# A ten-stage transformer block on one core: the first adaLN sums taken by TensorE, constants loaded later, zeroing products removed

## The chip, the cores and the metric

The kernel runs on one core of a Trainium2 chip. The metric is device time in microseconds (us) of one execution. All operands are fp32 in HBM.

## The reference, cut to what matters

Ten layers follow each other on a 256 x 1024 activation: FFN, Mamba-2, FFN, FFN, MoBA attention, FFN, stick-breaking attention, convolutional FFN, sparse (DSA) attention, convolutional FFN. Each is preceded by a modulated RMSNorm whose shift, scale and gate are a product of one vector with a large matrix:

```python
c_act = jax.nn.silu(c)                       # one vector of 1024
m = c_act @ w + b                            # w is 1024 x 3072, one per stage
shift, scale, gate = jnp.split(m, 3, axis=-1)
h = rmsnorm(x, g) * (1.0 + scale[:, None, :]) + shift[:, None, :]
x = x + 0.5 * gate * ((jax.nn.silu(h @ w_gate) * (h @ w_up)) @ w_down)
```

Every weight product is made at nearly fp32 accuracy: weights and activations are split into a high and a low part (fp32r), and three products hi*hi, hi*lo, lo*hi are summed.

## The kernel before, in words

**Layout.** x lies transposed in SBUF (`x`, 128 x 8 x 256). Weights come as 277 blocks of 1 MB (`raw0` to `raw5`, six buffers). For each block ScalarE writes `w_hi` (L421), VectorE writes `w_lo = raw - w_hi` (L817), two blocks ahead of TensorE (`AHEAD`), and TensorE makes 48 products (L1371 to L1373). A FFN takes gate block, up block, down block in turn (eleven of each); gate and up go to PSUM banks 4 and 5, the down products of the whole stage are summed in banks 0 to 3 (`acc(m)`, two to a bank).

**Start of a stage.** `norm(st)` on ScalarE squares x (L437), TensorE sums the squares with a matrix of ones (L1431, bank 6), ScalarE makes `rstd` (L425, L427), VectorE writes `work` (L908), ScalarE `h_hi` (L449), VectorE `h_lo` (L913). The first product of a stage runs as these land (L1384, L1386, then L1391). Between, TensorE zeroes banks 0 to 3 with four bf16 products of zeros (L1446, 128x512 each), so that all down products can accumulate. After the first gate product there is a small fp32 product into bank 6 that nobody reads (L1468).

**The modulation.** VectorE sums c times the 1024 rows of w in chunks of 128 rows (`macc`), for stages 1 to 9 in the background of FFN stages (L845, L848), then transposes (L828), reduces (L831) and TensorE folds (L1423). For stage 0 it is done at the start, before any weight product: eight chunks of 1 MB into `first_mod` (L345; the first four at once, each later one when the buffer is free), eight sums on VectorE (L1340, L1343), two transposes, two reductions, one small product, four additions (L875). The gate part of stage 0 comes later: four 0.5 MB pieces on ScalarE's queue (L411), summed in `first_gate` (L857 to L867).

**Queues.** All large loads are on SyncE's queue, in the order in which they are written: eight mods chunks with x (1 MB) before the last, `con` (all constants, 974 KB), six `raw` blocks, four mods chunks of the next stage, and then one `raw` per block freed. ScalarE's queue carries `par` (all parameters, 1189 KB) first, and later the gate pieces.

```python
            for n in range(KT):
                if n >= 4:
                    eng.wait_ge(sems["mo"], n - 3)
                eng.dma_start(first_mod[n % 4], mods[n][:, 0:2048]).then_inc(s_mo[n % 4], 16)
                if n == KT - 2:
                    eng.dma_start(x[:, :, :], xin).then_inc(s_in, 16)
            eng.dma_start(con[:, :], consts).then_inc(s_con, 16)
```

Of the kernel before, what the change touches and what calls it, by code (L numbers as in the profile page):

```python
# [71 lines left out]
PARAMS, NPARAM = offsets(PARAM_COLS)  # L72
CONSTS, NCONST = offsets(CONST_COLS)
# [49 lines left out]
class Plan:  # L123
# [20 lines left out]
    def steps(self, st, kind):  # L144
        g = GROUPS[kind]
        out = {"fold": 4, "mods": 1, "modv": 1, "pair": 3, "xup": 8, "sq": 8, "ss": 1, "ln": 1, "rstd": 1,
               "t": 8, "hhi": 8, "hlo": 8, "zero": 1, "ahi": 0, "alo": 0}
# [60 lines left out]
def build(nc, weights, mods, params, consts, xin, out, stages=None):  # L208
# [3 lines left out]
    with ExitStack() as ctx:  # L212
# [36 lines left out]
        turned_first = [modws[:, 3072:4608], modws[:, 4608:6144]]  # L249
# [9 lines left out]
        sems = {n: sem(n) for n in list(plan.total) + ["blk", "whi", "wlo", "macc", "const", "cact", "xst", "mo", "go", "gmods"]}  # L259
# [4 lines left out]
        s_in, s_par, s_con, s_out, s_rel, s_bias = (sem(n) for n in ("in", "par", "con", "out", "relst", "bias"))  # L264
# [19 lines left out]
        zero_b = conb[:, 3 * P:4 * P]  # L284
# [55 lines left out]
        def _(eng):  # L340
            k = Steps(eng, plan, sems)
            for n in range(KT):
                if n >= 4:
                    eng.wait_ge(sems["mo"], n - 3)
                eng.dma_start(first_mod[n % 4], mods[n][:, 0:2048]).then_inc(s_mo[n % 4], 16)  # L345
                if n == KT - 2:
                    eng.dma_start(x[:, :, :], xin).then_inc(s_in, 16)
            eng.dma_start(con[:, :], consts).then_inc(s_con, 16)

            def load(g):  # L350

                if g < plan.nblk:
                    if g >= NRAW:
                        eng.wait_ge(sems["wlo"], g - NRAW + 1)
                    eng.dma_start(raw[g % NRAW][:, :], weights[g]).then_inc(s_raw[g % NRAW], 16)

            def load_mod(q):

                if q < 16 * (NST - 1):
                    if q < 4:  # L360
                        eng.wait_ge(sems["fold"], 4)
# [5 lines left out]
            for g in range(NRAW):  # L367
                load(g)
            for q in range(4):
# [16 lines left out]
        def _(eng):  # L386
            k = Steps(eng, plan, sems)
            eng.dma_start(par[:, :], params).then_inc(s_par, 16)
            eng.wait_ge(s_par, 16)
            k.inc("cact", eng.activation(cact[:, :], par_("c"), ACT.Silu))  # L390

            def start():

                eng.wait_ge(s_con, 16)
                eng.activation(ident_b, con_("ident"), ACT.Copy)
# [5 lines left out]
                for b in range(-AHEAD, 0):  # L401
                    split(0, b=b)
                gate_weights(0)
# [25 lines left out]
            def norm(st):  # L429
# [10 lines left out]
                if st == 0:  # L440
                    start()
# [5 lines left out]
                for m in range(KT):  # L447
                    k.wait("t", st, b=m)
                    k.inc("hhi", eng.activation(h_hi[:, m, :], work3[:, m, :], ACT.Identity,  # L449
                                                bias=modv[:, st, m:m + 1]))  # L450

            def ffn(st):
# [23 lines left out]
                for n in range(1, NFB):  # L476
# [3 lines left out]
                    if st == 0 and n == GATE_AT:  # L480
                        gate_weights(1)
# [316 lines left out]
        def _(eng):  # L798
# [4 lines left out]
            eng.memset(zero_b, 0.0)  # L803

            def more_constants():
                eng.wait_ge(s_con, 16)
                eng.tensor_scalar(below_b, con_("tri"), 1.0, -NEG, ALU.subtract, ALU.mult).then_inc(sems["xst"], 1)
                eng.wait_ge(sems["const"], 1)
                eng.tensor_tensor(ws_lo[:, :], par_("wsmall"), ws_hi[:, :], ALU.subtract).then_inc(sems["xst"], 1)
# [9 lines left out]

            def fold(j, n):  # L820

                if n == 0:
                    eng.wait_ge(sems["macc"] if j else sems["mo"], 16 * j or KT)
                half, w = n % 2, 1536 if j else 1024
                flat = (turned if j else turned_first)[half][:, 0:w]
# [8 lines left out]
            def gather(st, n, step):  # L834
# [5 lines left out]
                for q in mod_parts(st, n, step):  # L840
                    m, c = macc[:, 1536 * (q % 2):1536 * (q % 2 + 1)], cact[:, KT + q // 2:KT + q // 2 + 1]
                    eng.wait_ge(s_modw[q % 4], 16 * (q // 4) + 16)
                    if q % 16 < 2:
                        k.wait("fold", q // 16, b=q % 2)
# [34 lines left out]
            def modulation(st):  # L879
# [3 lines left out]
                ins = tiles(st, 0, 24 if st else 16, 0)  # L883
                ins.then_inc(sems["xst"], 1)
                eng.wait_ge(sems["xst"], 2 + 2 * st + 1)
# [3 lines left out]
                eng.wait_ge(sems["xst"], 2 + 2 * st + 2)  # L889
# [64 lines left out]
            def ffn(st):  # L954
# [24 lines left out]
                for n in range(1, NFB):  # L979
# [4 lines left out]
                    if st == 0 and n in (GATE_AT, GATE_AT + 4):  # L984
                        first_gate((n - GATE_AT) // 4)
                    down(n, 3, 1)
# [350 lines left out]
            for n in range(KT):  # L1337
# [8 lines left out]
            for n in range(4):  # L1346
                fold(0, n)
# [577 lines left out]
```

## Time and profile before

| | us |
|---|---|
| median of 3 runs | 1853.33 (1853.1 to 1859.61) |
| the profiled execution, its time | 1857.99 |
| its span | 1856.2 |
| TensorE busy | 1754.0 |
| VectorE busy | 1444.3 |
| ScalarE busy | 962.0 |
| first weight product starts at | 40.53 |

The span runs from the first to the last instruction; the execution's own time is 1.8 us more. TensorE is busy for 94% of the span, so what the kernel can lose or gain is in the few places where it waits: the first 40 us, the starts of stages, and some stretches with much VectorE work. "PEclk" in the views is the clock granted to TensorE, 1.00 at 2.4 GHz and 0.50 at 1.2 GHz.

### The profile page before, as it was taken

To read this page: it belongs to the slowest core of one execution; us is meant where nothing else is said; L and a number is where in the kernel's file an instruction comes from. 1 tells how busy PE (TensorE), PEld (TensorE's weight loads), DVE (VectorE), ACT (ScalarE), POOL (GpSimd) and SP (SyncE) were. 2 spreads that over 40 slices of the span, in tenths; PEclk is the share of its full clock that TensorE was granted. 3 is DMA by queue.
4 is the path that set the end of the run, shared out by engine and by line. 5 is a ranking of instruction groups with operands and counts; after the bars stand their busy time and mean duration, and the time that the engine had idled before them with its cause. 6 is when DMAs were issued, how large, how long until landed. Compare 5 with 4: busy or idle time off the path is not lost.

```text
span 1856.2 us, 34083 instructions
## 1 busy us (share of the span) xinstructions
PE 1754.0 (94%) x14612; PEld 1693.6 (91%) x14612; DVE 1444.3 (78%) x1718; ACT 962.0 (52%) x1256; POOL 0.2 (0%) x4
## 2 busy tenths in 40 slices
PE   2998999999999999999989999999998999989999
PEld 2998989998899999999979999898898988889999
DVE  7799987877799879986547998655799777548676
ACT  3443465666544454435665344655644555656554
POOL 0000000000000000000000000000000000000000
PEclk9999999999999999999989999999999999999999
DMA  9998834343499859983435997243395544424551
GB/s 400 418 389 320 331 117 159 137 179 137 181 379 367 325 212 380 367 323 137 159 114 211 389 368 303 111 159 114 120 339 197 192 149 162 148 91 168 195 190 46
DMA packets 67278, 426.11 MB, mean 230 GB/s; under 512 B 7264, under 2 KB 10352, under 8 KB 30448
## 3 DMA queue, kind: packets, MB, share of 16 engines
q1 hardware_dynamic: 63216, 415.21, 58.8%
q10 hardware_dynamic: 3968, 9.63, 1.5%
q8 instruction: 61, 1.00, 0.2%
q14 instruction: 33, 0.27, 0.0%
HBM read 423.74 MB, written 3.17 MB: 230 GB/s over the span
## 4 chain that ended last, share of the span: by engine, by line
PE 83%; DVE 11%; ACT 3%; issue 2%; DMA 1%; SPq 0%; DVEq 0%; ACTq 0%
PE bank L1371 24%; PE bank L1372 23%; PE bank L1373 23%; DVE w_lo L817 4%; PE bank L1431 2%; DVE macc L848 2%; DMA modws<-mods 1%; PE bank L1384 1%; PE bank L1702 1%; PE bank L1386 1%; DVE mix L1003 1%; PE bank L1391 1%; ACT w_hi L421 1%; PE bank L1547 1%; DVE mix L828 1%
## 5 line engine op out<-in xcount | busy, mean ns | idle before, releaser
L1371 PE MATMUL bank<-h_hi,w_hi 128*128 128x256 f32 x2864 | 801.5, 280 | 15.5 <-DVE w_lo L817 14.6
L1373 PE MATMUL bank<-h_hi,w_lo 128*128 128x256 f32 x2864 | 794.7, 277 | 0.0
L1372 PE MATMUL bank<-h_lo,w_hi 128*128 128x256 f32 x2864 | 794.6, 277 | 0.0
L817 DVE TENSOR_TENSOR w_lo<-raw,w_hi 128x2048 fp32r<-128x2048 f32 x277 | 633.3, 2287 | 126.1 <-ACT w_hi L421 125.7
L421 ACT ACTIVATE w_hi<-raw 128x2048 fp32r<-128x2048 f32 x277 | 529.8, 1913 | 144.4 <-PE bank L1373 138.0
L1371 PEld LDWEIGHTS bank<-h_hi,w_hi 128*128 128x128 f32 x2864 | 539.9, 189 | 23.3 <-DVE w_lo L817 16.5
L1373 PEld LDWEIGHTS bank<-h_hi,w_lo 128*128 128x128 f32 x2864 | 539.9, 189 | 0.0
L1372 PEld LDWEIGHTS bank<-h_lo,w_hi 128*128 128x128 f32 x2864 | 539.6, 188 | 0.1
L1371 PE MATMUL bank<-a_hi,w_hi 128*128 128x256 f32 x1280 | 358.1, 280 | 0.0
L1372 PE MATMUL bank<-a_lo,w_hi 128*128 128x256 f32 x1280 | 355.0, 277 | 0.0
L1373 PE MATMUL bank<-a_hi,w_lo 128*128 128x256 f32 x1280 | 355.0, 277 | 0.0
L1371 PEld LDWEIGHTS bank<-a_hi,w_hi 128*128 128x128 f32 x1280 | 241.4, 189 | 1.8 <-issue 1.0
L1373 PEld LDWEIGHTS bank<-a_hi,w_lo 128*128 128x128 f32 x1280 | 241.6, 189 | 0.0
L1372 PEld LDWEIGHTS bank<-a_lo,w_hi 128*128 128x128 f32 x1280 | 241.3, 189 | 0.1
L848 DVE SCALAR_TENSOR_TENSOR macc<-modws,cact,macc 128x1536 f32<-128x1536 f32 x126 | 226.2, 1813 | 0.0
L1003 DVE SCALAR_TENSOR_TENSOR mix<-bank,par,mix 128x254 f32<-128x254 f32 (+1 forms) x176 | 76.7, 477 | 44.9 <-ACT mix L496 43.4
L471 ACT ACTIVATE a_hi<-mix 128x512 fp32r<-128x512 f32 x40 | 25.3, 632 | 148.8 <-PE bank L1373 111.5
L457 ACT ACTIVATE mix<-bank 128x512 f32<-128x512 f32 x44 | 26.3, 599 | 117.2 <-PE bank L1373 117.1
L496 ACT ACTIVATE mix<-bank,par 128x256 f32<-128x256 f32 x88 | 44.8, 559 | 75.7 <-PE bank L1373 75.4
L1431 PE MATMUL bank<-work,con 128*128 128x256 f32 x160 | 41.7, 399 | 32.2 <-DMA con<-consts 30.9
L1431 PEld LDWEIGHTS bank<-work,con 128*128 128x128 f32 x160 | 30.4, 201 | 36.9 <-DMA con<-consts 30.9
L1384 PE MATMUL bank<-h_hi,w_hi 128*128 128x256 f32 x160 | 41.2, 297 | 16.5 <-ACT h_hi L449 16.5
(258 smaller groups left out, 1647.5 us busy)
## 6 DMA issues: line engine op xcount, KB each, us to landing
raw<-weights SPq DMA_DIRECT2D x277, 1024.0 KB, 5.1
modws<-mods SPq DMA_DIRECT2D x144, 768.0 KB, 6.8
mix<-mods SPq DMA_DIRECT2D x6, 1024.0 KB, 8.0
mix<-mods ACTq DMA_DIRECT2D x8, 512.0 KB, 10.9
modws<-mods SPq DMA_DIRECT2D x2, 1024.0 KB, 12.0
biases<-scratch ACTq DMA_DIRECT2D x1, 2048.0 KB, 12.2
mix<-biases ACTq DMA_DIRECT2D x4, 512.0 KB, 4.0
par<-params ACTq DMA_DIRECT2D x1, 1189.0 KB, 8.0
```

Of the source, the lines that this page charges most:

```text
L421: eng.activation(w_hi[g % NW][:, :], raw[g % NRAW][:, :], ACT.Copy).then_inc(sems["whi"], 1)
L457: k.inc("silu", eng.activation(sg, bank[4][:, :].rearrange("p (a t) -> p a t", a=2), ACT.Silu))
L471: k.inc("ahi", eng.activation(z_hi if final else a_hi[:, :, :], act, ACT.Copy))
L496: ins = eng.activation(dst[:, m, :], b[:, m * T:(m + 1) * T], ACT.Identity, scale=cw(i, t, 2), bias=cw(i, t, 3))
L817: eng.tensor_tensor(w_lo[g % NW][:, :], raw[g % NRAW][:, :], w_hi[g % NW][:, :], ALU.subtract).then_inc(sems["wlo"], 1)
L848: ins = eng.scalar_tensor_tensor(out=m, in0=modw[q % 4], scalar=c, in1=m, op0=ALU.mult, op1=ALU.add)
L1003: ins = eng.scalar_tensor_tensor(out=dst[:, m, lag:T], in0=b[:, m * T:(m + 1) * T - lag], scalar=cw(i, 22 * up + m, tap), in1=dst[:, m, la ...
L1371: eng.matmul(dst, ah, bh, start=start, stop=False, skip_group_check=skip)
L1372: eng.matmul(dst, ah, bl, start=False, stop=False, skip_group_check=skip)
L1373: return eng.matmul(dst, al, bh, start=False, stop=stop, skip_group_check=skip)
L1384: eng.matmul(d, hi[:, kk, part], h_hi[:, kk, :], start=kk == m == 0, stop=False, skip_group_check=True)
L1431: mm = eng.matmul(bank[6][:, r * T:(r + 1) * T], con_("ones"), (sq2 if r else work3)[:, m, :], start=m == r == 0, stop=m == KT - 1, skip_g ...
```

## The change

- `consts` is loaded in two parts: the 128 columns of ones after the fourth mods chunk, the rest (910 KB) behind the sixth `raw` block. `params` in three: c alone, then what the norm needs, and the rest (985 KB) behind the rest of `consts`.
- The last two mods chunks of stage 0 come in halves, the scale half of both first. x is loaded before the sixth chunk.
- The sums over partitions of stage 0's modulation are made by TensorE: 16 products of a 128 x 128 piece of `macc` with one column of ones, instead of two transposes, two reductions, a product and four additions.
- The first weight block is loaded and split in halves; the second is split by ScalarE after `h_hi`.
- Constants of the later stages are made in stage 0's FFN (`mixer_constants`).
- The zeroing products go. The first down product into each bank has `start` set instead; for that the second iteration (i = 1) of each FFN loop is written out. In Mamba, the two products that write the decay rows of one bank change places.
- The small fp32 product of each FFN stage stays. In stage 0 it now has TensorE's wait for the rest of `consts` ahead of it.

```diff
@@ sync
-            for n in range(KT):
+            for n in range(KT - 2):
                 if n >= 4:
                     eng.wait_ge(sems["mo"], n - 3)
                 eng.dma_start(first_mod[n % 4], mods[n][:, 0:2048]).then_inc(s_mo[n % 4], 16)
-                if n == KT - 2:
+                if n == 3:
+                    eng.dma_start(con[:, 0:P], consts[:, 0:P]).then_inc(s_ones, 16)
+                if n == 4:
                     eng.dma_start(x[:, :, :], xin).then_inc(s_in, 16)
-            eng.dma_start(con[:, :], consts).then_inc(s_con, 16)
+            for n, (chunk, c) in enumerate(LATE_MODS):
+                eng.wait_ge(sems["mo"], chunk - 3)
+                eng.dma_start(first_mod[chunk % 4][:, c], mods[chunk][:, c]).then_inc(s_late_mod[n], 16)
...
             for g in range(NRAW):
                 load(g)
+            eng.dma_start(con[:, P:NCONST], consts[:, P:NCONST]).then_inc(s_con, 16)
+            eng.dma_start(par[:, PAR_HEAD:NPARAM], params[:, PAR_HEAD:NPARAM]).then_inc(s_par, 16)
@@ scalar
-            eng.dma_start(par[:, :], params).then_inc(s_par, 16)
-            eng.wait_ge(s_par, 16)
+            eng.dma_start(par[:, 0:PAR_C], params[:, 0:PAR_C]).then_inc(s_c, 16)
+            eng.dma_start(par[:, PAR_C:PAR_HEAD], params[:, PAR_C:PAR_HEAD]).then_inc(s_head, 16)
+            eng.wait_ge(s_c, 16)
...
-                    eng.wait_ge(sems["mo"], KT)
+                    eng.wait_ge(sems["mo"], 9)
...
+                if st == 0:
+                    split(0, b=1 - AHEAD)
+                    gate_weights(0)
@@ vector
+            def first_split():
+
+                for sem_, c in (("half", slice(0, 1024)), ("whi", slice(1024, 2048))):
+                    eng.wait_ge(sems[sem_], 1)
+                    ins = eng.tensor_tensor(w_lo[0][:, c], raw[0][:, c], w_hi[0][:, c], ALU.subtract)
+                ins.then_inc(sems["wlo"], 1)
...
-            for n in range(4):
-                fold(0, n)
-            more_constants()
-            split(0, b=-2)
+            for n, (chunk, cols) in enumerate(LATE_MODS):
+                eng.wait_ge(s_late_mod[n], 16)
+                eng.wait_ge(sems["mo"], KT - 2 + n)
+                for c in (slice(512, 1024), slice(0, 512)) if n == 3 else (cols,):
+                    eng.scalar_tensor_tensor(out=macc[:, c], in0=first_mod[chunk % 4][:, c],
+                                             scalar=cact[:, chunk:chunk + 1], in1=macc[:, c],
+                                             op0=ALU.mult, op1=ALU.add).then_inc(sems["mo"], 1)
+            first_split()
             modulation(0)
@@ tensor
+            def first_modulation():
+
+                for n in [*range(8, 16), *range(4, 8), *range(4)]:
+                    eng.wait_ge(sems["mo"], 8 if n >= 8 else 10 if n >= 4 else 11)
+                    mm = eng.matmul(bank[7][:, n:n + 1], macc[:, n * P:(n + 1) * P], con_("ones")[:, 0:1],
+                                    start=True, stop=True)
+                k.inc("mods", mm)
...
-                    modulation(0)
-                    eng.wait_ge(sems["const"], 1)
-                    eng.wait_ge(sems["xst"], 2)
-                else:
-                    k.wait("xup", st - 1, b=7)
-                for n in range(4):
-                    mm = eng.matmul(bank[n][:, :].rearrange("p (a c) -> p a c", a=4), ident_b,
-                                    zero_b.unsqueeze(1).to_broadcast([P, 4, P]), start=True, stop=True)
-                k.inc("zero", mm)
+                    first_modulation()
...
                 gate(0, 0, 0, True)
+                if st == 0:
+                    eng.wait_ge(s_con, 16)
                 eng.matmul(bank[6][:, 0:96], con_("ones"), con_("tri")[:, 0:96], start=True, stop=True)
                 up(0, 0, 1, True)
-                for i in k.loop(1, NFB - 1):
+                gate(1, 3, -1)
+                up(1, 3, 0)
+                down(1, 3, 1, True)
+                for i in k.loop(2, NFB - 1):
```

SyncE's queue at the start of the program, before: mods chunks (`mix`, `modws`), x, all of `con`, then the `raw` blocks.

```order
L345 DMA mix<-mods 128x2048 x3
L345 DMA modws<-mods 128x2048
L345 DMA mix<-mods 128x2048 x3
L347 DMA x<-xin 128x2048
L345 DMA modws<-mods 128x2048
L348 DMA con<-consts 128x1948
L355 DMA raw<-weights 128x2048 x6
L365 DMA modws<-mods 128x1536 x4
```

The same queue after the change:

```order
L350 DMA con<-consts 128x128
L348 DMA mix<-mods 128x2048
L352 DMA x<-xin 128x2048
L348 DMA mix<-mods 128x2048
L355 DMA mix<-mods 128x1024
L355 DMA modws<-mods 128x1024
L355 DMA mix<-mods 128x1024
L355 DMA modws<-mods 128x1024
L363 DMA raw<-weights 128x1024
L364 DMA raw<-weights 128x1024
L366 DMA raw<-weights 128x2048 x5
L380 DMA con<-consts 128x1820
```

The bulk of `con` moved from ahead of the six blocks to behind them, and `par`'s rest (L381) stands behind it.

TensorE between stage 0 and stage 1, before: the last sums of squares (L1431), the zeroing products, the first gate product.

```order
L1431 MATMUL bank<-work,con 128x256 [waits s_sq] x6
L1446 MATMUL bank<-conb 128x512 [waits s_xup]
L1446 MATMUL bank<-conb 128x512 x3
L1384 MATMUL bank<-h_hi,w_hi 128x256 [waits s_hhi,s_wlo]
L1386 MATMUL bank<-h_hi,w_lo 128x256
```

After the change, at the same place:

```order
L1415 MATMUL bank<-h_hi,w_lo 128x256
L1479 MATMUL bank<-work,con 128x256 [waits s_sq] x6
L1426 MATMUL bank<-h_hi,w_hi 128x256 [waits s_hhi,s_wlo]
L1428 MATMUL bank<-h_hi,w_lo 128x256
```

Nothing stands between the sums and the wait for `h_hi` (`s_hhi`) now. And TensorE's place in stage 0 after the first gate product (its last rows L1433), where the small product now waits for `s_con`:

```order
L1433 MATMUL bank<-h_lo,w_hi 128x256 [waits s_hlo]
L1433 MATMUL bank<-h_lo,w_hi 128x256
L1510 MATMUL bank<-con 128x96 [waits s_con]
L1413 MATMUL bank<-h_hi,w_hi 128x256 [waits s_wlo]
L1414 MATMUL bank<-h_lo,w_hi 128x256
```

The up product (L1413 on) is queued behind that wait.

## Rows read from the trace of the kernel before

**Rows 1.** The chain that ended last, 28 to 49 us: start, us, what.

```profile
28.50 2.36 DVE macc L1343
...
30.88 2.37 DVE modws L828 x2
...
36.01 2.20 DVE w_lo L817
...
39.36 3.26 DVE work L908 x8
...
45.78 2.21 DVE w_lo L817
...
48.04 0.38 PE bank L1371
```

**Rows 2.** Timeline of all engines, 0 to 130 us: start, us, instruction, idle before.

```profile
18.55 7.33 DVE L1343 SCALAR_TENSOR_TENSOR macc<-mix,cact,macc 128x2048 f32<-128x2048 f32 x3
...
35.81 1.81 ACTq L411 DMA_DIRECT2D mix<-mods  x4
...
40.53 0.36 PE L1384 MATMUL bank<-h_hi,w_hi 128*128 128x256 f32 x1 [2.47 <-ACT h_hi L449]
```

**Rows 3.** DMAs of single lines: duration ns, issue times; then us to landing.

```profile
L348 SPq DMA_DIRECT2D con<-consts x1: 433/433/433, 18.8 to 18.8; - x1
...
DMA to landing us min/median/max: 12.0/12.0/12.0
...
L355 SPq DMA_DIRECT2D raw<-weights x6: 432/432/432, 19.3 to 21.7; - x6
...
DMA to landing us min/median/max: 14.0/19.4/27.3
```

**Rows 4.** Busy time in one stretch; last columns PEclk, DMA share, GB/s.

```profile
20.00:40.00 20.00, 7.20 (x22) 5.35 (x22) 16.86 (x19) 8.73 (x17) 0.00 (x0) 1.00 1.01 421
```

**Rows 5.** VectorE's timeline in stage 0: four sums over 128x1024.

```profile
132.28 5.24 DVE L860 SCALAR_TENSOR_TENSOR work<-mix,cact,work 128x1024 f32<-128x1024 f32 x4
```

**Rows 6.** Timeline at the start of stage 1.

```profile
232.99 2.75 PE L1431 MATMUL bank<-work,con 128*128 128x256 f32 x12
...
235.58 1.03 PE L1446 MATMUL bank<-conb 128*128 128x512 bf16 x4
...
237.91 0.36 PE L1384 MATMUL bank<-h_hi,w_hi 128*128 128x256 f32 x1 [1.30 <-ACT h_hi L449]
```

**Rows 7.** Waits of the whole span: us in total, times, longest.

```profile
PE bank L1384 <- ACT h_hi L449: 16.5, 10, 3.7
```

**Rows 8.** TensorE's timeline: first instruction after three of its idle stretches.

```profile
964.84 1.40 PE L1702 MATMUL bank<-mix 128*64 128x256 f32 x4 [2.17 <-ACT mix L655]
...
1295.33 1.15 PE L1674 MATMUL bank<-mix,con 128*128 128x256 f32 x2 [2.15 <-DVE work L1217]
...
1654.06 0.70 PE L1702 MATMUL bank<-mix 128*128 128x256 f32 x2 [2.08 <-ACT mix L655]
```

**Rows 9.** Stretches that follow an idle TensorE, columns as rows 4.

```profile
40.50:44.00 3.50, 3.47 (x30) 3.50 (x31) 3.50 (x10) 3.48 (x8) 0.00 (x0) 1.00 1.03 421
...
237.90:243.00 5.10, 5.09 (x43) 5.10 (x44) 5.10 (x14) 4.47 (x8) 0.00 (x0) 1.00 0.00 0
...
964.80:974.00 9.20, 7.99 (x34) 6.26 (x35) 1.98 (x9) 5.10 (x7) 0.00 (x0) 0.50 0.01 2
...
1176.50:1182.70 6.20, 6.13 (x29) 6.17 (x30) 6.20 (x17) 4.52 (x8) 0.00 (x0) 0.50 0.00 0
...
1295.40:1298.80 3.40, 3.40 (x12) 2.96 (x13) 2.52 (x7) 1.66 (x4) 0.00 (x0) 0.50 0.00 0
...
1654.10:1658.00 3.90, 3.87 (x24) 3.06 (x25) 0.42 (x1) 2.01 (x5) 0.00 (x0) 1.00 0.00 0
```

**Rows 10.** Timeline, stage 0: where VectorE has the backlog.

```profile
148.14 1.92 ACT L421 ACTIVATE w_hi<-raw 128x2048 fp32r<-128x2048 f32 x1 [4.91 <-PE bank L1373]
158.18 0.63 ACT L471 ACTIVATE a_hi<-mix 128x512 fp32r<-128x512 f32 x1 [8.12 <-DVE mix L963]
```

More of the change, by code:

```diff
@@ L145, in steps @@
         g = GROUPS[kind]
-        out = {"fold": 4, "mods": 1, "modv": 1, "pair": 3, "xup": 8, "sq": 8, "ss": 1, "ln": 1, "rstd": 1,
-               "t": 8, "hhi": 8, "hlo": 8, "zero": 1, "ahi": 0, "alo": 0}
+        out = {"fold": 4 if st else 0, "mods": 1, "modv": 1, "pair": 3, "xup": 8, "sq": 8, "ss": 1, "ln": 1, "rstd": 1,
+               "t": 8, "hhi": 8, "hlo": 8, "ahi": 0, "alo": 0}
         if st == RESCALED:
@@ L257, in sem @@
             return ctx.enter_context(nc.semaphore("s_" + name))
-        sems = {n: sem(n) for n in list(plan.total) + ["blk", "whi", "wlo", "macc", "const", "cact", "xst", "mo", "go", "gmods"]}
+        sems = {n: sem(n) for n in list(plan.total) + ["blk", "whi", "wlo", "macc", "const", "cact", "xst", "late", "mo", "go", "gmods", "half"]}
         s_raw = [sem(f"raw{s}") for s in range(NRAW)]
@@ L263, in build @@
         s_modw = [sem(f"modw{s}") for s in range(4)]
-        s_in, s_par, s_con, s_out, s_rel, s_bias = (sem(n) for n in ("in", "par", "con", "out", "relst", "bias"))
+        s_in, s_c, s_head, s_par, s_ones, s_con = (sem(n) for n in ("in", "c", "head", "par", "ones", "con"))
+        s_out, s_rel, s_bias, s_raw_half = (sem(n) for n in ("out", "relst", "bias", "raw_half"))
+        s_late_mod = [sem(f"late_mod{n}") for n in range(4)]
         def view(off, *dims):
@@ L354, in load @@
                         eng.wait_ge(sems["wlo"], g - NRAW + 1)
+                    if g == 0:
+                        eng.dma_start(raw[0][:, 0:1024], weights[0][:, 0:1024]).then_inc(s_raw_half, 16)
+                        eng.dma_start(raw[0][:, 1024:2048], weights[0][:, 1024:2048]).then_inc(s_raw[0], 16)
+                        return
                     eng.dma_start(raw[g % NRAW][:, :], weights[g]).then_inc(s_raw[g % NRAW], 16)
@@ L480, in ffn @@
                     if st == 0 and n == GATE_AT:
+                        mixer_constants()
                         gate_weights(1)
@@ L843, in gather @@
                     if q % 16 < 2:
-                        k.wait("fold", q // 16, b=q % 2)
+                        if q < 2:
+                            k.wait("mods", 0)
+                        else:
+                            k.wait("fold", q // 16, b=q % 2)
                         ins = eng.tensor_scalar(m, modw[q % 4], c, None, ALU.mult)
@@ L985, in ffn @@
                         first_gate((n - GATE_AT) // 4)
+                    if st == 0 and n == GATE_AT + 1:
+                        mixer_constants()
                     down(n, 3, 1)
@@ L1336, in _ @@
             eng.wait_ge(sems["cact"], 1)
-            for n in range(KT):
+            for n in range(KT - 2):
                 eng.wait_ge(s_mo[n % 4], 16 * (n // 4 + 1))
@@ L1413, in gemm_out @@
                         mm = three(acc(m), hi[:, kk, part], lo[:, kk, part], a_hi[:, kk, :], a_lo[:, kk, :],
-                                   False, False, True)
+                                   fresh and kk == m % 2 == 0, False, True)
                 mm.then_inc(sems["blk"], 1)
+            def first_modulation():
[4 more added lines that the diff above has]
+                k.inc("mods", mm)
             def modulation(st):
                 k.wait("fold", st, b=3)
-                if st:
-                    k.wait("modv", st - 1)
-                w = 96 if st else 64
-                k.inc("mods", eng.matmul(bank[7][:, 0:w], con_("fold"), folded[st % 3][:, 0:w], start=True, stop=True))
+                k.wait("modv", st - 1)
+                k.inc("mods", eng.matmul(bank[7][:, 0:96], con_("fold"), folded[st % 3][:, 0:96], start=True, stop=True))
             def squares(st, pair):
@@ L1487, in last @@
                 if st == 0:
+                    eng.wait_ge(sems["const"], 1)
+                    eng.wait_ge(sems["late"], 2)
                     eng.wait_ge(sems["go"], KT + 2)
@@ L1744, in body @@
                         gemm_out(st, i, a, b + (2 if kind == "dsa" else 3),
-                                 lambda kk: k.wait("alo", st, i, 2, kk - 2))
+                                 lambda kk: k.wait("alo", st, i, 2, kk - 2), i == 1)
                 if kind == "dsa":
```

61 lines of the change are left out of this document (34 added, 27 removed).

## The prediction

> **What bounds the kernel now.** I read the busy time by engine first (the table of the profile): TensorE works 1754.0 of 1856.2 us, so an edit counts only where TensorE waits or where its clock falls. The waits of TensorE come next. Its longest is the start, with nothing to multiply before 40.53 us [rows 2]. After that the ten starts of a stage hold 16.5 us together, the longest 3.7 [rows 7]. The chain of waits then says what the start waits for [rows 1]: the last 1 MB of mods (landed at 28.50), its sum on VectorE (2.36), two transposes (2.37), two reductions (up to 35.5), the split of block 0 (36.01, 2.20), the norm from 39.36, and, after the first gate product, the split of block 1 from 45.78, until the up product starts at **48.04**. Behind it TensorE runs block after block until VectorE falls behind after 132 us. So 48.04, not 40.53, is the time that everything later hangs on. The view by stretches says one thing more: the DMA engines are full (share 1.01, 421 GB/s) in those 20 to 40 us [rows 4]. Whatever is loaded later than before stands in a full queue.
>
> **The start, step by step.** Durations are those of the profiled execution.
>
> *Up to the first gate product.* The last mods chunk no longer has 985 KB of `par` beside it. At 421 GB/s [rows 4] a block of 1024 KB takes 2.5 us and the 985 KB 2.4, so it lands at about 26.1. But VectorE is then late. x now goes ahead of the sixth chunk, which so is the seventh transfer; the seventh landed two transfers ahead of 28.5, at 23.5, now less 2.4: 21.1. Until then VectorE waits (it finished the seventh chunk at 25.9 before [rows 2]). From there 2.4 for the sixth chunk, three halves of 1.31 (5.24 for four [rows 5]) and two quarters of 0.7: 28.8, with the gaps between them 29.1. The folds go (4.6 us, 30.88 to 35.5), and so do 0.6 of constants. The split of block 0 comes next on VectorE in two halves, 2.3: 31.4. TensorE's 16 one-column products lie beside it. No row here shows such a product at the low clock; at 0.2 to 0.45 us each the last four end between 30 and 34 us, and I take the lower end. With 0.7 for `modv` and `gs` the norm starts at 32.1 instead of 39.36, and the first gate product at 40.53 - 7.2 = 33.3. Its split of block 1 would be done at 48.0 - 7.2 = 40.8.
>
> *The new wait.* The small product after it needs the rest of `con`. It lands today at 18.8 + 12.0 = 30.8 [rows 3]. Now it stands behind six blocks: + 6 x 2.5 = 15.0, less 2.4 for `par`: 43.4. The gate pieces share the DMA engines with it. ScalarE issues them at 35.81 today [rows 2] and would at about 35.3, behind `h_hi`. Today the six blocks land from 19.3 + 14.0 = 33.3 to 21.7 + 27.3 = 49.0 [rows 3], 15.7 us for five blocks where 12.5 are needed without the gate pieces: 3.2 lost in the 9 us from 40 on. For the 4 us behind 39.3 that is, at this rate of a third and more, some 2.1: **con lands at 45.5** (bounds 43.4 with no sharing, 47.2 if they halve each other). Queued behind this wait is the up product. It starts at 45.9 instead of 48.04: a gain of 2.1 (4.2 to 0.4), not 7.2. VectorE's split of block 1 (40.8) is no longer what is late; ScalarE's `silu` and all later splits have three blocks of lead and are not either.
>
> *The clock after that wait.* The gate product ends at 39 (full clock) to 42 (low clock), so TensorE idles for 4 to 6 us. After the idle 3.66 us at stage 6 the granted clock is 0.50, the 1.2 GHz level, for all of 1176.5 to 1182.7 [rows 9]; the short case is 3.4 us (1295.40 to 1298.80). Half speed for 3.4 us loses 1.7, for 6.2 it loses 3.1. I take 1.7. **The start: 2.1 - 1.7 = 0.4 gained**, bounds 4.2 gained and 2.7 lost.
>
> **Stage 0 after it.** VectorE falls behind at 132 us (the four gate sums, then the folds) and TensorE waits there: ScalarE's `a_hi` waits 8.12 us for VectorE [rows 10]. That chain hangs on TensorE's own products before it, so it moves with them: 0. The later constants, six short instructions that stood at the start, now lie beside the second and third iteration, where TensorE is what the splits wait for, as `w_hi` does for 4.91 us at 148 [rows 10]: 0; with no cover about 1. The four mods chunks of the next stage and block 6 stand behind the same bytes as today: 0.
>
> **The zeroing products.** Each of ten stages issues four, 1.03 us [rows 6]. At stage 1 the last sum of squares ends at 235.7, the zeroing ends at 236.6, and TensorE then still waits 1.30 for `h_hi`. The chain ss, `rstd`, `work`, `h_hi` does not touch them, so removing them starts nothing earlier: 0, at most 9 x 1.03 = 9.3 if it did. The one written-out iteration and the swapped pair in Mamba issue the same products: 0, plus or minus 1.
>
> *But the idle gap grows* from 1.30 to 2.33 us at eight of the nine later starts (16.5 in all = 2.47 + 3.66 + 8 x 1.30 [rows 7]; 3.66 becomes 4.7, where the clock falls already). After 1.30 us the clock stayed at 1.00, the 2.4 GHz level, each time (stage 1 stands for eight: 237.90 to 243.00 at 1.00 [rows 9]). The trace has four gaps between 2 and 2.5 us: after 2.17 (964.84) and 2.15 (1295.33) it fell to 0.50, after 2.08 (1654.06) and 2.47 (40.53) it did not [rows 2, 8, 9]. So a start with 2.33 falls about one time in two. One fall loses 1.7 us, since the gate and up products behind it run without waits (43 products in 5.10 us). I leave out stage 7, where VectorE is late afterwards. **7 x 0.5 x 1.7 = 6.0 lost**, bounds 0 and 8 x 1.7 = 13.6.
>
> The Trainium skill ("TensorE: Matmul & The Clock Gate", section "Why this matters for your kernels") advises to have no idle gaps over some 3 us between bursts of matmuls. By that rule the 2.33 us would cost nothing and the sum would be 0.4 faster; the rows with 2.15 and 2.17 speak against it, and I go by them.
>
> **The sum.** -0.4 + 6.0 = +5.6 on the profiled execution's own 1857.99 (its span 1856.2 and 1.8 around it): 1863.6. That execution lay 4.7 above the median of the runs, 1853.33; against the median the same change gives **1859**.
>
> **The rivals.**
>
> A. *The clock holds at the stage starts.* 2.33 us behaves like the 2.47 at 38 us. For it: that gap. Against: 2.15 and 2.17. Time: 1853.33 - 0.4 = 1853. The advice of the Trainium skill above would have it so.
>
> B. *The start keeps its gain.* `con` lands before it is missed, or what waits for it costs little; the up product moves by the full 7.2 with the clock high. For it: the lower bound of the DMA sum (43.4) and a VectorE chain that is shorter by all the folds. Against: the full DMA engines [rows 4]. With the falls half there 1853.33 - 7.2 + 6.0 = 1852, with none 1846.
>
> C. *The zeroing products were on the path.* 9.3 and 0.4 gained: 1844. Against: the wait of 1.30 behind them.
>
> D. *Slower: the clock falls at nearly every start.* Place: the gate product of stages 1 to 5 and 7 to 9; price 1.7 each, 3.1 where the low clock lasts 6.2 us; it passes the bound from six of eight on (6 x 1.7 = 10.2). All eight and nothing gained at the start: 1853.33 + 13.6 = 1867. For it: all gaps from 3.6 us on fell, and these come nearer to them. Against: 2.47 did not.
>
> **How the numbers follow.** A measurement of this kernel can tell 0.5% from no change, 9.3 us: below 1844.1 is faster, above 1862.6 slower. Chances: the forecast 0.47 (its own range 1855 to 1863), A 0.22, B 0.10, C 0.04, D 0.17. The range 1847 to 1867 takes in A, most of B and D up to all eight falls, and leaves out C and longer low stretches. Faster: C and the best of B, 0.07. Slower: D and the upper tail of the forecast, 0.19. Same: 0.74.
>
> **What would show it.** Right: the first gate product near 33 us; the next product released by the DMA of `con` at 45 to 46; low clock behind it; a wait of 2.3 us at eight starts of a stage with PEclk 0.5 behind about four of them. Wrong: a wait at the up product that names `w_lo`, at about 41; PEclk at 1.00 behind the 2.3 us waits, or below it behind all of them; a gap that is still 1.3 us; new waits of VectorE for `modws` or of ScalarE for `raw` in stage 0, which would mean that the full queue takes the gain back.

## The result, and the profile after

| | before | after |
|---|---|---|
| median, us | 1853.57 (10 runs, 1851.18 to 1864.83) | **1880.06** (10 runs, 1863.94 to 1889.29) |
| ratio | | 1.0122, 95% interval 1.0088 to 1.0155 |
| the profiled execution, us | 1857.99 | 1883.62 |
| its span, us | 1856.2 | 1881.8 |
| mean granted clock | 0.991 | 0.978 |

The change makes the kernel 1.2% slower; 1.0122 is the estimate from all runs of both kernels, the two medians alone stand at 1.014. One execution of a later experiment (e4) took 2950 us at a mean granted clock of 0.556; it isn't explained, and e4's ratio leaves it out. I had forecast 1859 and a range up to 1867, so the result lies outside it. The page of the kernel after, busy time by engine and the clock in 40 slices:

```profile
PE 1784.9 (95%) x14602; PEld 1729.5 (92%) x14602; DVE 1441.1 (77%) x1714; ACT 961.6 (51%) x1257; POOL 0.2 (0%) x4
...
PEclk8999999998999999999999999999999999999999
```

TensorE does ten instructions fewer than before and is busy 30.9 us longer (1754.0 before). So the loss is not idle time: TensorE takes longer over the same products.

**The start** went as forecast. The timeline of the kernel after, all engines (start, us, instruction, idle before and what ended it):

```profile
26.69 1.95 PE L1463 MATMUL bank<-con,macc 128*128 128x1 f32 x16 [0.47 <-DVE macc L1388]
...
28.93 3.57 PE L1463 MATMUL bank<-con,macc 128*128 128x1 f32 x16 [0.30 <-DVE macc L1388]
...
33.22 3.25 DVE L944 SCALAR_TENSOR_TENSOR work<-x,gs,rstd 128x256 f32<-128x256 f32 x8
...
34.39 0.55 PE L1426 MATMUL bank<-h_hi,w_hi 128*128 128x256 f32 x1 [1.89 <-ACT h_hi L468]
...
46.42 0.74 PE L1510 MATMUL bank<-con 128*128 128x96 f32 x2 [4.07 <-DMA con<-consts]
46.87 0.56 PE L1413 MATMUL bank<-h_hi,w_hi 128*128 128x256 f32 x1
```

and in the view by stretches (columns as in rows 4) the low clock behind that wait:

```profile
46.50:49.40 2.90, 2.90 (x14) 2.90 (x15) 0.61 (x1) 0.00 (x0) 0.00 (x0) 0.50 1.02 414
```

The first gate product starts 6.1 us earlier than in [rows 2], the up product 1.2 us earlier than the 48.04 of [rows 1], and the clock takes that back: stage 1 starts at 238.04, before at 237.91 [rows 6].

**The starts of stages.** TensorE's timeline at stage 1, which answers to [rows 6], and the wait of the whole span that answers to [rows 7]:

```profile
234.63 1.24 PE L1479 MATMUL bank<-work,con 128*128 128x256 f32 x5
238.04 0.36 PE L1426 MATMUL bank<-h_hi,w_hi 128*128 128x256 f32 x1 [2.16 <-ACT h_hi L468]
```

```profile
PE bank L1426 <- ACT h_hi L468: 23.7, 10, 4.5
```

23.7 = 1.89 (stage 0) + 4.5 (stage 6) + eight of 2.16 or 2.17, where there were eight of 1.30. The clock behind them, by stretches, for stages 1, 2, 3, 4, 5, 7, 8, 9:

```profile
238.10:243.70 5.60, 5.60 (x49) 5.55 (x49) 5.54 (x15) 4.41 (x8) 0.00 (x0) 1.00 0.00 0
479.50:482.90 3.40, 3.40 (x18) 3.40 (x18) 3.40 (x10) 3.37 (x6) 0.00 (x0) 0.51 0.01 2
672.30:677.90 5.60, 5.60 (x48) 5.60 (x49) 5.20 (x14) 5.57 (x9) 0.00 (x0) 1.00 0.02 4
858.50:861.80 3.30, 3.30 (x16) 3.30 (x17) 3.30 (x10) 3.30 (x8) 0.00 (x0) 0.50 0.00 0
988.20:991.50 3.30, 3.30 (x17) 3.30 (x17) 3.30 (x10) 3.28 (x7) 0.00 (x0) 0.50 0.00 0
1329.50:1332.80 3.30, 3.30 (x18) 3.30 (x17) 3.30 (x9) 3.27 (x7) 0.00 (x0) 0.50 0.00 0
1534.30:1537.60 3.30, 3.30 (x17) 3.30 (x17) 3.30 (x9) 3.13 (x5) 0.00 (x0) 0.50 0.00 0
1691.30:1694.60 3.30, 3.30 (x18) 3.30 (x17) 3.30 (x10) 3.27 (x6) 0.00 (x0) 0.50 0.02 5
```

Six of eight at 0.50, the 1.2 GHz level. Each lasts 3.4 us and loses 1.7, so 10.2 us. That is less than half of 25.6.

**The rest is a pace.** Take three stretches inside the FFN stages 2, 3 and 5, with the clock at 1.00 and TensorE without a pause in them (us, TensorE's busy time and count first). Before:

```profile
500.00:655.00 155.00, 155.00 (x1369) 155.00 (x1368) 139.69 (x94) 64.96 (x48) 0.00 (x0) 1.00 0.90 355
695.00:842.00 147.00, 147.00 (x1271) 147.00 (x1270) 132.15 (x82) 59.14 (x45) 0.00 (x0) 1.00 0.90 348
1020.00:1160.00 140.00, 140.00 (x1237) 140.00 (x1236) 127.17 (x82) 57.47 (x44) 0.00 (x0) 1.00 0.89 353
```

After:

```profile
500.00:655.00 155.00, 155.00 (x1319) 155.00 (x1318) 136.78 (x84) 60.86 (x45) 0.00 (x0) 1.00 0.90 348
695.00:842.00 147.00, 147.00 (x1299) 147.00 (x1298) 134.77 (x84) 61.03 (x46) 0.00 (x0) 1.00 0.91 360
1020.00:1160.00 140.00, 140.00 (x1191) 140.00 (x1191) 126.84 (x78) 55.20 (x43) 0.00 (x0) 1.00 0.90 350
```

155 us over 1369 products is 113.2 ns per product, 155 / 1319 is 117.5; 140 us give 113.2 and 117.5; 147 / 1299 is 113.2. The same product, at the same granted clock, with 128 x 128 weights and 256 columns, has two paces, **113.3 and 117.6 ns** from one start to the next (below: quick and slow; the counts take in the products that the edges of a stretch cut, which makes the quotients some 0.1 ns too small). Before is quick in stages 2, 5, 7, 9 and in the first half of stage 3 (x1271 lies between). After is slow in 2, 5, 7, 9 and quick in 3; only stage 7 isn't steady, it is quick from 1393 to 1428, between two waits for `w_lo`. A FFN stage has 33 blocks of 48 products: 1584 x 4.3 ns = 6.8 us. The lengths, from one first gate product to the next (stage 9: to the end of the span):

| stage | before | after | clock after | pace, before / after |
|---|---|---|---|---|
| 2 | 186.2 | 194.2 | fell | quick / slow |
| 3 | 189.4 | 186.2 | held | quick, then slow / quick |
| 5 | 192.1 | 200.0 | fell | quick / slow |
| 7 | 198.8 | 204.5 | fell | quick / slow, quick from 1393 to 1428 |
| 9 | 183.6 | 191.7 | fell | quick / slow |

The four that fell grew by 8.0, 7.9, 5.7 and 8.1: 29.7, of which 6.8 is low clock in the gate product. The other 23 is pace in stages 2, 5 and 9 (6.2 to 6.4 each). In stage 7 it is less, and part of it is a second low stretch behind a wait, 6.8 us long at 1432 where before has 3.4 at 1422. Stage 3 gave 3.2 back, the start and the other stages (0, 1, 4, 6, 8) together 1.0.

### The profile page after: what moved, and what is told of

Read it like the earlier page. It is cut to its first block, busy times and chain, and to the rows that moved or that the text cites. A ratio compares the mean times of both kernels' runs of the same rounds, so it can differ in the third digit from the quotient of the medians.

```text
span 1881.8 us, 34045 instructions
## 1 busy us (share of the span) xinstructions
PE 1784.9 (95%) x14602; PEld 1729.5 (92%) x14602; DVE 1441.1 (77%) x1714; ACT 961.6 (51%) x1257; POOL 0.2 (0%) x4
## 4 chain that ended last, share of the span: by engine, by line
PE 84%; DVE 9%; ACT 3%; DMA 2%; issue 2%; SPq 0%; DVEq 0%; ACTq 0%
PE bank L1413 24%; PE bank L1414 24%; PE bank L1415 24%; DVE w_lo L839 3%; PE bank L1479 2%; DVE macc L880 2%; PE bank L1426 1%; DMA con<-consts 1%; PE bank L1428 1%; PE bank L1749 1%; DVE mix L1041 1%; PE bank L1433 1%; DMA modws<-mods 1%; PE bank L1591 1%; PE bank L1730 1%
## 5 line engine op out<-in xcount | busy, mean ns | idle before, releaser
L1413 PE MATMUL bank<-h_hi,w_hi 128*128 128x256 f32 x2864 | 809.0, 282 | 12.5 <-DVE w_lo L839 11.7
L1413 PEld LDWEIGHTS bank<-h_hi,w_hi 128*128 128x128 f32 x2864 | 546.8, 191 | 17.0 <-DVE w_lo L839 13.1
L1413 PE MATMUL bank<-a_hi,w_hi 128*128 128x256 f32 x1280 | 360.6, 282 | 0.0
L1413 PEld LDWEIGHTS bank<-a_hi,w_hi 128*128 128x128 f32 x1280 | 243.4, 190 | 1.8 <-issue 1.0
L1426 PE MATMUL bank<-h_hi,w_hi 128*128 128x256 f32 x160 | 51.5, 346 | 23.7 <-ACT h_hi L468 23.7
L1426 PEld LDWEIGHTS bank<-h_hi,w_hi 128*128 128x128 f32 x160 | 40.3, 252 | 27.1 <-issue 27.1
```

The lines of the kernel that those rows point to most:

```text
L1413: eng.matmul(dst, ah, bh, start=start, stop=False, skip_group_check=skip)
L1426: eng.matmul(d, hi[:, kk, part], h_hi[:, kk, :], start=kk == m == 0, stop=False, skip_group_check=True)
```

## The experiments

Two theories were open. *Structure*: the written-out iteration or the earlier start makes the products slow. *Clock*: a fall of the clock in the gate product leaves the stage slow. The small product of each FFN stage (L1468 before, L1510 after) stands right behind the gate product, so it was under suspicion too. Nothing reads it, so its removal changes no output. In the same way a copy of it, or a zeroing product more, adds nothing to the output. In the views an fp32 product counts as two instructions (`x2`), one of bf16 or of the weights as one. The pace is read from one profiled execution of each kernel, the times from all of them.

**e1. The changed kernel with the zeroing products back at stages 1 to 9.**

```diff
+                else:
+                    k.wait("xup", st - 1, b=7)
+                    for n in range(4):
+                        eng.matmul(bank[n]..., ident_b, zero_b..., start=True, stop=True)
```

> The changed kernel with the four zeroing products back at the start of stages 1 to 9 (their results are overwritten), everything else as changed. Theory P (pace): TensorE runs its 256-column products at one of two paces at full clock, 113.3 or 117.6 ns; the small fp32 product turns the one into the other, and a fall and rise of the clock inside the gate product changes which one it meets. With the idle gap back at about 1.2 us the clock no longer falls at the starts, FFN stages run at 113.3 and the time is about 1851 (1848 to 1856). Theory S (structure: the written-out iteration or the start flags set the slow pace): about 1880, PEclk high but 117.6 in stages 2, 5, 7, 9. Theory L (only the time at the low clock costs): about 1853, and the same pace as before in every stage.

Measured: 1858.72, ratio to before 1.0002 (0.9982 to 1.0023). The loss is gone, though each zeroing costs TensorE 1.03 us. TensorE's timeline at stage 2, and the pace there:

```profile
481.68 1.03 PE L1494 MATMUL bank<-conb 128*128 128x512 bf16 x4
484.01 0.36 PE L1428 MATMUL bank<-h_hi,w_hi 128*128 128x256 f32 x1 [1.30 <-ACT h_hi L469]
```

```profile
500.00:655.00 155.00, 155.00 (x1370) 155.00 (x1369) 140.56 (x88) 64.98 (x48) 0.00 (x0) 1.00 0.90 354
```

No fall at any of the eight starts, and stages 2, 3, 5, 7, 9 all quick behind the small product. The written-out iteration is still there, so structure is out. That it isn't faster than before is stage 0: slow for about half its length after the wait for `con`, with the clock low from 45.2 to 52.1, and 209.4 us long (197.4 before).

**e2. The kernel before with only the zeroing taken out** (the L1446 products gone, `start` on the first down product, the second iteration written out for that; start of the program as before).

```diff
-                for n in range(4):
-                    mm = eng.matmul(bank[n]..., ident_b, zero_b..., start=True, stop=True)
-                k.inc("zero", mm)
...
-                for i in k.loop(1, NFB - 1):
+                gate(1, 3, -1)
+                up(1, 3, 0)
+                down(1, 3, 1, True)
+                for i in k.loop(2, NFB - 1):
```

> The kernel before with only the zeroing products removed (start flag in the first down product, second FFN iteration written out), its prologue as it was. Theory P: the gaps at the starts are 2.2 to 2.4 us, the clock falls at most of them, and the FFN stages where it fell run at 117.6: about 1878 (1865 to 1888). Theory L: only falls of 1.7 us each, 1860 to 1866. If the start of the program were to blame: about 1853.

Measured: 1893.82, ratio 1.0200 (1.0183 to 1.0217), above my range. One edit alone brings the loss, more of it than the whole change. The three stretches:

```profile
500.00:655.00 155.00, 155.00 (x1318) 155.00 (x1318) 138.20 (x88) 63.29 (x47) 0.00 (x0) 1.00 0.90 348
695.00:842.00 147.00, 147.00 (x1250) 147.00 (x1250) 132.48 (x83) 59.62 (x45) 0.00 (x0) 1.00 0.91 355
1020.00:1160.00 140.00, 140.00 (x1191) 140.00 (x1190) 126.82 (x79) 56.50 (x42) 0.00 (x0) 1.00 0.93 362
```

Here the clock fell in all five FFN stages from 2 on and in stage 0, and all are slow behind the small product, stage 0 up to 146 and stage 7 up to 1407, the others to their last block.

**e3. The kernel before without the small product** (L1468 deleted), and **e4. the changed kernel without it** and without its wait for `con`.

```diff
-                if st == 0:
-                    eng.wait_ge(s_con, 16)
-                eng.matmul(bank[6][:, 0:96], con_("ones"), con_("tri")[:, 0:96], start=True, stop=True)
```

> The kernel before without the small fp32 product, whose result nobody reads, in all FFN stages. Theory P: stages 2, 3, 5, 7, 9 enter the gate product at the slow pace and nothing turns it: 117.6 throughout, 1536 products x 4.3 ns = 6.6 us each, 33 less the 3 us that stage 3 loses already: about 1883 (1875 to 1890). Theories L and S: 1852 to 1853, as the product costs 0.2 us or nothing.

> The changed kernel without the small fp32 product (and without the wait for the rest of con ahead of it in stage 0). Theory P: now it is the FFN stages where the clock fell in the gate product that are quick (113.3), and those where it did not fall that are slow (117.6): with four of five falling about 1860 to 1864 from the pace, less 4 us that stage 0 gains as the up product no longer waits for con: 1858 (1850 to 1868). Theory S: as changed, 1876 to 1880. Theory L: 1876.

Measured: e3 1881.04, ratio 1.0127 (1.0106 to 1.0147); e4 1867.36, ratio 1.0044 (1.0018 to 1.0070). e3 takes one short product out of six stages and loses 24 us, with the clock at 1.00 all the while:

```profile
500.00:655.00 155.00, 155.00 (x1318) 155.00 (x1317) 136.68 (x86) 62.77 (x47) 0.00 (x0) 1.00 0.91 351
695.00:842.00 147.00, 147.00 (x1251) 147.00 (x1250) 132.76 (x83) 58.46 (x43) 0.00 (x0) 1.00 0.92 357
1020.00:1160.00 140.00, 140.00 (x1191) 140.00 (x1190) 128.20 (x79) 54.75 (x42) 0.00 (x0) 1.00 0.92 354
```

So the pace needs no fall to be slow, and the small product does something. In e4 it is the other way round: stages 2, 3 and 7 (7 up to a wait that ends at 1418) are quick behind a fall, 5 is slow behind one. In e4 the up product follows the gate product at 41.94, without a pause, and stage 1 starts at 231.7: the start is worth 6.2 us once nothing waits for `con`.

**e5. e1 without the small product of stage 0 and its wait**, and **e8. the same with 16 zeroing products at stage 6** (second hunk).

```diff
-                if st == 0:
-                    eng.wait_ge(s_con, 16)
-                eng.matmul(bank[6][:, 0:96], con_("ones"), con_("tri")[:, 0:96], start=True, stop=True)
+                if st:
+                    eng.matmul(bank[6][:, 0:96], con_("ones"), con_("tri")[:, 0:96], start=True, stop=True)
@@ e8 only
-                    for n in range(4):
+                    for n in [*range(4)] * (4 if st == RESCALED else 1):
```

> The changed kernel with the zeroing products back (as in the first experiment) and, in stage 0 alone, without the small fp32 product and its wait for the rest of con. Theory P: the up product of stage 0 starts at about 42 instead of 46.4 to 47 and stage 0 keeps the quick pace, since the clock rises inside its gate product and nothing turns the pace after it; stage 1 starts at about 232 (as it did without the product) and everything behind it as in the first experiment, 1612.7 us from there: 1846 (1843 to 1851). If the DMA queue or VectorE took the earlier start back: 1853 to 1856.

> As the fifth experiment, with sixteen zeroing products instead of four at the start of stage 6, where TensorE idles 3.66 us behind them: 12 x 0.26 us more fill leave a gap of about 0.6. The clock should not fall there: 3 us less at the low clock, 1843 (1840 to 1848). If the products are not what keeps the clock up, it falls as before and the time is that of the fifth experiment.

Measured: e5 **1846.55**, ratio 0.9950 (0.9931 to 0.9969); e8 **1845.40**, ratio 0.9945 (0.9922 to 0.9968). Both beat both kernels; their intervals overlap, so the times don't tell e8 from e5. The profiled execution of e5 (1851.14) isn't what I expected of it: stage 0 is slow up to 138, and stage 1 starts at 236.72. In that of e8 (1842.08) stage 0 is quick and stage 1 starts at 231.94. In e8 the wait at stage 6, 3.66 before, ends after 1.07 with the clock at 1.00, and the stage takes 137.8 us, in e5 141.1 (the view shows 13 of the 16 products):

```profile
1160.62 2.97 PE L1494 MATMUL bank<-conb 128*128 128x512 bf16 x13
1164.66 0.36 PE L1428 MATMUL bank<-h_hi,w_hi 128*128 128x256 f32 x1 [1.07 <-ACT h_hi L469]
```

**e6 and e7. The small product twice in a row**, in the kernel before and in the changed one. If each turned the pace, two would leave it.

```diff
                 eng.matmul(bank[6][:, 0:96], con_("ones"), con_("tri")[:, 0:96], start=True, stop=True)
+                eng.matmul(bank[6][:, 0:96], con_("ones"), con_("tri")[:, 0:96], start=True, stop=True)
```

> The kernel before with the small fp32 product issued twice in a row in every FFN stage. If the product turns the pace over (theory P): turned twice, so stages 2, 3, 5, 7, 9 run at 117.6 as without it, about 1881 (1875 to 1888). If the product sets the quick pace whatever it was before, or if its presence as such is what counts: about 1856.

> The changed kernel with the small fp32 product twice. If it turns the pace over: like the changed kernel without it, quick where the clock falls and slow where it does not; 1866 (1858 to 1875), with the wait for con still there. If it sets a pace, or merely takes time: as the changed kernel, 1876 to 1882.

Measured: e6 1856.50, ratio 0.9992 (0.9970 to 1.0013); e7 1876.52, ratio 1.0097 (1.0061 to 1.0134). Two in a row act like one. I took that as the end of the theory that the product turns the pace. It was not, see e11.

**e9 and e10. Another product in its place**, in the kernel before: bf16 operands (e9), 256 columns (e10).

```diff
-   eng.matmul(bank[6][:, 0:96], con_("ones"), con_("tri")[:, 0:96], start=True, stop=True)
+   eng.matmul(bank[6][:, 0:96], ident_b, zero_b[:, 0:96], start=True, stop=True)             # e9
+   eng.matmul(bank[6][:, 0:256], con_("ones"), con[:, 0:256], start=True, stop=True)         # e10
```

> The kernel before, with the small product of each FFN stage (con x con, 128x96, fp32, one instruction) done on bf16 operands of the same shape. It works out nothing that the output needs. Theory 'it takes an fp32 product': the FFN stages 2, 3, 5, 7, 9 run at 117.5 ns per 256-column product as they do with none, and the kernel takes 1881. Theory 'any product of another width does it': the stages stay at 113.3 ns, 1857.

> The kernel before, with the small fp32 product of each FFN stage made 256 columns wide in place of 96. Theory 'it takes an fp32 product': stages 2, 3, 5, 7, 9 at 113.3 ns, 1857 to 1859 (the wider product costs some 0.3 us a stage more). Theory 'the odd width (96 columns) does it': 117.5 ns and 1881.

Measured: e9 1863.58, ratio 1.0024 (1.0003 to 1.0046); e10 1861.65, ratio 1.0014 (0.9998 to 1.0030). Neither type nor width is the point: e10 has stages 2, 3, 5, 9 quick and only 7 slow at first, and e9's stages are quick in part. But e9 has stages 2, 5, 7 quick and 3, 9 slow with no fall at all, which "a fall makes it slow" can't explain. What tells them apart is the pace *ahead* of the small product. The last 16 products of the gate product are one row, and 15 steps and the last one's 0.28 us make 2.05 at the slow pace and 1.98 at the quick one. In the changed kernel, stage 3 (clock held, then quick) and stage 5 (clock fell, then slow):

```profile
676.09 2.05 PE L1433 MATMUL bank<-h_lo,w_hi 128*128 128x256 f32 x16
...
993.17 1.98 PE L1433 MATMUL bank<-h_lo,w_hi 128*128 128x256 f32 x16
```

It is opposite to what follows. So the product may turn the pace after all, and a fall matters because the products that follow it are mostly quick.

**e11. e2 with the small product once more, 96 products later**; **e12. the same in the changed kernel.**

```diff
                 gate(1, 3, -1)
+                eng.matmul(bank[6][:, 0:96], con_("ones"), con_("tri")[:, 0:96], start=True, stop=True)
                 up(1, 3, 0)
```

> The kernel before without the zeroing products (as e2), with the same small fp32 product once more in each FFN and convolutional FFN stage, between the gate and the up product of the second iteration. In e2 the stages 2, 3, 5, 7, 9 came at 118 ns from the first small product on, 1893.8 in all. Theory 'a small product turns the pace to the other of the two': from the second one on these stages run at 113 ns; 5 stages and stage 0 save some 6 us each, 1857 to 1863. Rival 'the pace is set at the start of the stage, by the clock': 1894 as before, all stages at 118.

> The changed kernel, with the same second small product in the second iteration. Theory 'turns': stages in which the clock fell in the gate product (six or so) run quick from the second iteration on, those in which it did not run slow; 4 x -6.5 and 1 x +6.5 against 1880: about 1861. Rival 'set at the start': 1880, the same stages slow as in the changed kernel.

Measured: e11 1878.42, ratio 1.0105 (1.0077 to 1.0133), 15 us less than e2. e12 1876.88, ratio 1.0096 (1.0062 to 1.0129). TensorE's timeline of e11 around the second small product of stage 3 (L1465):

```profile
692.10 0.28 PE L1373 MATMUL bank<-h_hi,w_lo 128*128 128x256 f32 x1
692.22 0.28 PE L1371 MATMUL bank<-h_hi,w_hi 128*128 128x256 f32 x1
692.34 0.28 PE L1372 MATMUL bank<-h_lo,w_hi 128*128 128x256 f32 x1
692.46 0.28 PE L1373 MATMUL bank<-h_hi,w_lo 128*128 128x256 f32 x1
692.58 0.36 PE L1465 MATMUL bank<-con 128*128 128x96 f32 x2
692.72 0.36 PE L1371 MATMUL bank<-h_hi,w_hi 128*128 128x256 f32 x1
```

Ahead of it the steps are 0.12 us; the rest of the stage, and that of the others, in the same three stretches:

```profile
500.00:655.00 155.00, 155.00 (x1318) 155.00 (x1318) 136.66 (x85) 61.69 (x46) 0.00 (x0) 1.00 0.90 352
695.00:842.00 147.00, 147.00 (x1299) 147.00 (x1298) 134.69 (x83) 60.79 (x46) 0.00 (x0) 1.00 0.92 365
1020.00:1160.00 140.00, 140.00 (x1238) 140.00 (x1237) 128.48 (x81) 59.04 (x44) 0.00 (x0) 1.00 0.91 363
```

x1250 of e2 has become x1299 and x1191 x1238. Stages 3, 5, 7 and 9, slow behind the first product, are quick behind the second. Stage 2, where the clock happened to hold and the first left it quick, is slow behind the second. In e12 the second turned 5 and 9 to quick and 2, 3 and 7 to slow. That is ten of ten FFN stages turned in one or the other direction. The totals were forecast too low (1857 to 1863, and 1861). Stages that needed no turning were turned as well, one in e11 and three in e12, where I had counted one. And in e11 stage 7, from which I had counted 6 us, gave none (201.7 us, 200.1 in e2): in e2 it was slow only up to 1407. It is the pace behind each product, not the sum, that decides between the theories.

All profiled executions together, stages 2, 3, 5, 7, 9 of before, after and e1 to e12, by the pace of the gate product's last 16 and of the products behind the small one:

| gate product | clock in it | small product | behind it |
|---|---|---|---|
| slow | held / fell | one or two | quick 31 of 31 (28 / 3) |
| quick | fell | one or two | slow 17 of 17 |
| quick | held | one or two | quick 8, slow 4 |
| either | either | none (e3, e4) | unchanged 8, slow after quick 2 |

In the third row, and in the two of the last row that changed, one step ahead of the gate product's last product is 0.1 us longer than the others (their row of 16 takes 2.08 to 2.10). In those two nothing but that longer step stands between the quick and the slow products.

**Turns without the small product.** The traces hold more of them. In stage 7 of the changed kernel the load of a weight waits 0.3 us for `w_lo` at full clock:

```profile
1392.19 0.28 PE L1414 MATMUL bank<-a_lo,w_hi 128*128 128x256 f32 x1
1392.31 0.28 PE L1415 MATMUL bank<-a_hi,w_lo 128*128 128x256 f32 x1
1392.67 0.39 PE L1413 MATMUL bank<-h_hi,w_hi 128*128 128x256 f32 x1
1392.90 0.28 PE L1414 MATMUL bank<-h_lo,w_hi 128*128 128x256 f32 x1
```

The step of 0.36 us turns slow to quick (24 steps ahead of 1391 take 117.8 ns on average, 24 from 1394 on 113.3). In stage 3 of the kernel before one step of 0.15 us, at 757.81, turns quick to slow (767 in 86.6 us ahead, 723 in 84.9 behind). And in stage 0 of e5 and of e4, where the up product follows the gate product with nothing between, first e5:

```profile
41.60 0.39 PE L1435 MATMUL bank<-h_lo,w_hi 128*128 128x256 f32 x2
41.86 0.39 PE L1415 MATMUL bank<-h_hi,w_hi 128*128 128x256 f32 x1
42.09 0.28 PE L1416 MATMUL bank<-h_lo,w_hi 128*128 128x256 f32 x1
```

```profile
41.71 0.39 PE L1433 MATMUL bank<-h_lo,w_hi 128*128 128x256 f32 x2
41.94 0.28 PE L1413 MATMUL bank<-h_hi,w_hi 128*128 128x256 f32 x1
42.06 0.28 PE L1414 MATMUL bank<-h_lo,w_hi 128*128 128x256 f32 x1
```

Both come quick. Behind e5's joint, 0.15 us longer in all, the 90 us from 45 hold 766 products (slow), behind e4's even one 791 (quick). Over the fourteen traces I count 155 waits or longer steps in the weight products at full clock with no other product between and an even pace on both sides: of 30 out of the slow pace 16 turned, of 125 out of the quick one 30. So the small product is one interruption of the stream among others. It turned the pace far more often than these (48 of 48 where the gate product was slow, or was quick behind a fall).

## Why the prediction was wrong

**The start: right.** First gate product 34.4 (33.3), `con` 46.4 (45.5), up product 46.87 (45.9), low clock behind it 3.4 us (3.4). The up product moved by 1.2 us (2.1). Gained at stage 1: -0.1 (0.4). The 1.1 us between 33.3 and 34.4 are the one-column products, the last of which ends at 32.5 where I had taken 30 out of 30 to 34. Rival B's gain comes only where the wait for `con` is absent and stage 0 is quick (stage 1 starts at 231.69 in e4, at 231.94 in e8; at 236.72 in e5, where it is slow).

**The zeroing products themselves: right.** Their removal started nothing earlier; the gap took their place, 2.16 for the 2.33 forecast (rival C, 1844, is out). The rest of stage 0 and the later constants cost nothing that the trace shows (197.4 + 6.1 = 203.5 against 203.6).

**How often the clock falls: half right.** I said one start in two; it was six of eight here. Over the six profiled executions without zeroing (after, e2, e4, e7, e11, e12) 34 of 48 starts with a gap of 2.16 us fell, and none of 64 with 1.30 (before, e1, e3, e5, e6, e8, e9, e10). At the price I had, six falls and -0.1 for the start give 1853.33 + 0.1 + 10.2 = 1864.

The Trainium skill ("TensorE: Matmul & The Clock Gate", "Why this matters for your kernels") advises against idle gaps over some 3 us, and by that advice these would cost nothing. Here 2.16 us were followed by a fall in 34 of 48 cases, so the measurement decides against it.

**The step that failed is "One fall loses 1.7 us".** I priced a fall by the low clock alone and took it that products behind it cost what they cost before. Of a fall in an FFN stage the low clock is 1.7 us, and (29.7 - 6.8) / 4 = 5.7 more comes behind it, nearly all of it slow pace: the fall leaves the gate product quick (20 of the 24 that fell, all traces together), and the small product turns that to slow. Four such stages make 23 of the 25.6 us. With their 29.7, the 3.4 of the two other falls and stage 3's -3.2 the sum would have been 1853.33 + 0.1 + 29.9 = 1883, where 1880.06 was measured. I had also left out stage 7, as VectorE is late there; its clock fell too, and it grew by 5.7. "The same products: 0" for the untouched stages failed with it. The row to see it was there: before itself changes pace in stage 3 at 758. A mean of 280 ns per product in a table by line hides it, since that is each product's own length and not the step to the next.

The pace, as an interplay of the fall and the small product, is shown by e1, e2, e3 and e11. What stays open is why TensorE has two paces, and what in an interruption turns them. For the small product it isn't the type (e9) nor the width (e10), and two in a row act as one (e6, e7); short waits turn the pace as well, but not each time, and none was put in on purpose. How many stages are slow may also be what spreads the times of one kernel (1863.94 to 1889.29 after the change); one trace for each kernel can't show it.

## What to carry to other kernels

Count products per us in a stretch of full clock, before and after: a kernel that streams the same product for 1.8 ms can lose 1.3% by its step alone (e3), and neither the clock nor the waits show it (TensorE's busy time does, 30.9 us more here, without saying where). Products that do no work can hold the clock through a wait that would be there anyway: the four zeroing products, 1.03 us each time, kept eight gaps at 1.30 us with no fall, and started no gate product later (from the first of stage 0's last sums to stage 1's gate product it is 4.92 us with them and without). Look too for what hangs on a product that does no work: here the kernel that keeps the zeroing and drops the one wait for `con` (e5, e8) is 0.5% faster than before, where the whole change is 1.2% slower.

## What the runs showed of the hardware that was not expected

- Two steady paces of weight load and 256-column product at a granted clock of 1.00, 113.3 and 117.6 ns, each kept for over 150 us at a time. The Trainium skill ("TensorE: Matmul & The Clock Gate", "Wait — 56ns, not 53.3ns?") gives columns / 2.4 GHz and some 2.5 ns for back-to-back products, an estimate of 109.2 ns here; both paces are above it. At the low clock it gives columns / 1.2 GHz, 213 ns, and the trace of the changed kernel agrees: ten steps from 47.23 to 49.36 us, 213 ns each.
- One small product between them turns the one pace to the other: ten of ten in e11 and e12. A wait of 0.3 us, or a step 0.04 us longer than the others, can do it too (46 of 155).
- A one-column fp32 product on 128 x 128 weights, two instructions: 1.95 / 8 = 0.24 us at full clock, 3.57 / 8 = 0.45 where it was mostly low.
